# Two hybrid layers in a new order: convolution first, modulation chunks between weight chunks, attention woven into the triangular inverse

## The reference

```python
mod = jax.nn.silu(c) @ ada_w + ada_b          # 6 x 1024 shifts, scales and gates
h = rms_norm(x, norm_mix) * (1 + sc_m) + sh_m
(aq, ak, av, bq, bkc, bvc, bks, bvs, bkw, bvw, bg, cqkv, cz, ca, cb) = jnp.split(h @ w_in, points, axis=-1)
o_a = banded_attention(rope(aq), rope(ak), av, 128, attn_sinks)        # 4 heads of 64
o_b = nsa_mixer(...)    # compressed, selected and window branches, 4 heads of 64, gated by bg
o_c = gated_delta_net(cqkv, ca, cb, cz, conv_w, A_log, dt_bias, gdn_norm)   # 4 heads of 128
x = x + gt_m * (jnp.concatenate([o_a, o_b, o_c], axis=-1) @ w_out)
```

## Time and profile before

| | |
|---|---|
| median of 3 runs | 1755.29 us (1745.7 to 1759.51) |
| profiled execution | 1758.94 us |
| its span, first to last instruction | 1757.1 us |
| TensorE busy | 1564.1 us, 89% |
| TensorE weight loads | 1470.0 us, 84% |
| VectorE busy | 1031.5 us, 59% |
| ScalarE busy | 785.3 us, 45% |
| GpSimd busy | 273.1 us, 16% |
| mean granted TensorE clock | 0.934 of 2.4 GHz |
| first and second hybrid layer's stretch | 43.1 to 273.2 and 534.5 to 758.0 us |

### The profile page before, as it was taken

The page is one execution under the profiler, slowest core; times in us unless marked ns, Lnnn a source line. Parts: engine busy times, 40 slices in busy tenths (PEclk is TensorE's granted clock), DMA queues, the critical chain, the costliest instruction groups (busy, mean ns, idle before and its releaser), DMA issues.

```text
span 1757.1 us, 29189 instructions
## 1 busy us (share of the span) xinstructions
PE 1564.1 (89%) x12266; PEld 1470.0 (84%) x12266; DVE 1031.5 (59%) x1324; ACT 785.3 (45%) x1178; POOL 273.1 (16%) x102
## 2 busy tenths in 40 slices
PE   5899798989898986989999899569999999999997
PEld 2886487989898864879999799448999988889997
DVE  1575536795664765367554533685876454478743
ACT  3335423434234354334533444354664355556642
POOL 0000255570530002554000000220000001100000
PEclk8997798999999988999999899679999999999999
DMA  8358324554453470244445734203553543245442
GB/s 362 145 218 314 122 97 165 205 205 176 180 195 144 180 285 41 97 152 157 176 156 180 258 144 158 96 1 101 187 191 133 198 172 133 98 154 175 161 151 88
DMA packets 30190, 287.82 MB, mean 164 GB/s; under 512 B 2887, under 2 KB 11367, under 8 KB 11784
## 3 DMA queue, kind: packets, MB, share of 16 engines
q1 hardware_dynamic: 28888, 269.51, 41.9%
q0 software_dynamic: 1152, 16.78, 2.4%
q10 hardware_dynamic: 48, 0.05, 0.0%
HBM read 285.23 MB, written 7.39 MB: 167 GB/s over the span
## 4 chain that ended last, share of the span: by engine, by line
PE 72%; DVE 16%; ACT 4%; issue 4%; DMA 3%; POOL 1%; SPq 0%; DVEq 0%; ACTq 0%
PE bank L623 20%; PE bank L624 19%; PE bank L625 19%; DVE w_lo L1676 4%; DMA ring<-w_mix 3%; PE bank L703 2%; DVE arena L1997 2%; ACT w_hi L1253 1%; PE bank L846 1%; PE bank L748 1%; PE bank L836 1%; DVE h L2118 1%; PE bank L844 1%; PE bank L738 1%; PE bank L761 1%
## 5 line engine op out<-in xcount | busy, mean ns | idle before, releaser
L623 PE MATMUL bank<-hi_T,w_hi 128*128 128x256 f32 x2248 | 653.3, 291 | 41.3 <-DVE h_lo L1659 16.4
L1676 DVE TENSOR_TENSOR w_lo<-ring,w_hi 128x2048 fp32r<-128x2048 f32 (+2 forms) x218 | 515.2, 2373 | 229.7 <-ACT w_hi L1253 228.0
L625 PE MATMUL bank<-hi_T,w_lo 128*128 128x256 f32 x2248 | 647.3, 288 | 0.0
L624 PE MATMUL bank<-h_lo,w_hi 128*128 128x256 f32 x2056 | 592.0, 288 | 0.0
L1253 ACT ACTIVATE w_hi<-ring 128x2048 fp32r<-128x2048 f32 (+3 forms) x226 | 391.8, 1735 | 349.6 <-PE bank L625 278.5
L623 PEld LDWEIGHTS bank<-hi_T,w_hi 128*128 128x128 f32 x2248 | 444.1, 198 | 47.7 <-issue 34.8
L625 PEld LDWEIGHTS bank<-hi_T,w_lo 128*128 128x128 f32 x2248 | 443.7, 197 | 0.0
L624 PEld LDWEIGHTS bank<-h_lo,w_hi 128*128 128x128 f32 x2056 | 405.8, 197 | 0.3
L623 PE MATMUL bank<-act_hi,w_hi 128*128 128x256 f32 x704 | 201.3, 286 | 11.7 <-DVE act_lo L1695 9.9
L624 PE MATMUL bank<-act_lo,w_hi 128*128 128x256 f32 x704 | 200.4, 285 | 0.0
L625 PE MATMUL bank<-act_hi,w_lo 128*128 128x256 f32 x704 | 200.3, 284 | 0.0
(11 more groups left out here) (234 smaller groups left out, 2014.6 us busy)
## 6 DMA issues: line engine op xcount, KB each, us to landing
ring<-w_gu SPq DMA_DIRECT2D x22, 2048.0 KB, 8.4
ring<-w_dn SPq DMA_DIRECT2D x32, 1408.0 KB, 6.0
ring<-w_up SPq DMA_DIRECT2D x22, 2048.0 KB, 8.1
ring<-ada SPq DMA_DIRECT2D x16, 2048.0 KB, 8.2
ring<-w_mix SPq DMA_DIRECT2D x12, 2048.0 KB, 8.2
arena<-ada POOLq DMA_DIRECT2D x8, 2048.0 KB, 9.5
ring<-even_in SPq DMA_DIRECT2D x8, 2048.0 KB, 8.3
ring<-odd_in SPq DMA_DIRECT2D x6, 2048.0 KB, 8.3
```

Source lines behind the costliest of these rows:

```text
L623: nc.tensor.matmul(out, wh, xh, start=start, stop=False)
L624: nc.tensor.matmul(out, wh, xl, start=False, stop=False)
L625: return nc.tensor.matmul(out, wl, xh, start=False, stop=stop)
L1676: V.tensor_tensor(w_lo[:, n % SLOTS, at], ring[:, n % SLOTS, at], w_hi[:, u % AHEAD, 0:size].bitcast(F32), ALU.subtract).then_inc(w_lo_rea ...
```

## The change

In both hybrid layers the order is new; the sums computed are the same. The projection is split in `conv{l}` (three chunks for the convolution, now first), `tok{l}`, and `in{l}` (two chunks of attention tiles, and z); the weight columns are permuted on the host to fit. A modulation chunk follows each of the six big chunks, and none is left behind the projection. ScalarE writes the first (rightmost) tap while it takes a convolution tile from PSUM, so that VectorE runs three taps. The convolved rows are transposed between halves of chunks; ScalarE makes the sums of squares and the product with beta from PSUM, where VectorE did. The operand steps move from attention to the projection. Attention's units run inside the seven levels: in level lv TensorE transposes unit lv, and after the updates of X it does the values of unit lv and the scores of unit lv + 2. Scores and transposes of a unit now both use banks 4 and 5. The compression products come behind the projection. The core of the diff, in the order of the file (TensorE, ScalarE, VectorE, GpSimd, host):

```diff
+CN_FIRST, V1_FIRST = 162, 112
...
-    IN_ADA = (2, 4)
     UP, DOWN, OUT = ["columns"] * 11, ["down"] * 8, ["columns"] * 2
     ada_chunks(ADA_FIRST)
     for l in range(L1):
-        phase(f"in{l}", ["columns"] * 5 + ["tokens"], ada_after=IN_ADA)
+        phase(f"conv{l}", ["columns"] * 3, ada_after=(0, 1, 2))
         phase(f"tok{l}", ["rows"], KT * TOKW // 2)
+        phase(f"in{l}", ["columns"] * 2 + ["tokens"], ada_after=(0, 1, 2))
         phase(f"cmp{l}", ["compress"] * 2)
-        ada_chunks(4)
         phase(f"out{l}", OUT)
...
+                U["bank"] = 2 if woven else 4 if name.startswith("hybrid") else 2 * ((len(units) + i) % 2)
...
+                if m >= ADA_FIRST:
+                    pe.wait_ge(acc_ready, m)
...
+                elif U["bank"] == 4:
+                    first = stages["hybrid0"][0] if u < stages["hybrid0"][1] else stages["hybrid1"][0]
+                    if u:
+                        pe.wait_ge(logits_done, u)
+                    if u - first >= 2:
+                        pe.wait_ge(pt_ready, u - 1)
...
+                if units[u]["bank"] == 4:
+                    pe.wait_ge(logits_done, min(u + 2, stages["hybrid0" if u < stages["hybrid0"][1] else "hybrid1"][1]))
...
+            def rotate(l, t):
+
+                pe.wait_ge(gemm_freed, phases[f"in{l}"]["t0"] + t + 1)
+                if t < 2:
+                    pe.wait_ge(gt_copied, 13 * l + 6)
+                elif t < 4:
+                    pe.wait_ge(rope_done, 7 * l + t - 1)
+                else:
+                    pe.wait_ge(g_arg, 3 * l + 3)
+                nc.tensor.matmul(bank[:, 4 + t % 2, 0:S], const("rot"), raw[:, t, :], start=True, stop=True)\
+                    .then_inc(rot_ready, 1)
...
+            def input_columns(l, ready):
+
+                m = ADA_L * l + ADA_FIRST
+                conv_name, name, src = f"conv{l}", f"in{l}", (hi_T, h_lo)
+                columns_chunk(conv_name, 0, 0, src, ready)
+                ada_dots(m)
+                columns_chunk(conv_name, 1, 4, src)
+                ada_dots(m + 1)
+                modulations(m, m + 1)
+                columns_chunk(conv_name, 2, 8, src, parts=(0,))
+                if l == 0:
+                    pe.wait_ge(consts_in, 16 * 2)
+                token_major(l, 0)
+                columns_chunk(conv_name, 2, 8, src, parts=(1,))
+                ada_dots(m + 2)
+                modulations(m + 1, m + 2)
+
...
+                token_major(l, 1)
+
+                columns_chunk(name, 0, 0, src, first_bank=2, parts=(0,))
+                token_major(l, 2)
+                columns_chunk(name, 0, 0, src, first_bank=2, parts=(1,))
+                ada_dots(m + 3)
+                modulations(m + 2, m + 3)
+                rotate(l, 0)
+                rotate(l, 1)
+                columns_chunk(name, 1, 4, src, first_bank=2, parts=(0,))
+                rotate(l, 2)
+                rotate(l, 3)
+                columns_chunk(name, 1, 4, src, first_bank=2, parts=(1,))
+                ada_dots(m + 4)
+                modulations(m + 3, m + 4)
+                log_decays(l)
+                tokens_chunk(name, 2, 8, 2, parts=(0,))
+                rotate(l, 4)
+                rotate(l, 5)
+                tokens_chunk(name, 2, 8, 2, parts=(1,))
+                ada_dots(m + 5)
+                modulations(m + 4, m + 5)
...
+            def mixing(l):
+
+                m = ADA_L * l + ADA_FIRST
+                u0 = stages[f"hybrid{l}"][0]
+
+                pe.wait_ge(xpe_ready, 2 * (l + 1))
+                pe.wait_ge(acc_ready, m + 6)
...
+                    if lv == 1:
+                        modulations(m + 5, m + 6)
+                    transposes(u0 + lv)
...
+                    if lv == 0:
+                        pe.wait_ge(kc_ready, l + 1)
+                    values(u0 + lv)
+                    if lv + 2 < len(range(*stages[f"hybrid{l}"])):
+                        scores(u0 + lv + 2)
...
+            def take_conv(l, t):
+
+                act.wait_ge(gemm_ready, phases[f"conv{l}"]["tile_event"][t])
+                nc.scalar.activation(conv_in[:, t, 3:3 + S], bank[:, t % 4, 0:S], ACT.Copy)
+                nc.scalar.activation(conv[:, t, :], bank[:, t % 4, 0:S], ACT.Copy,
+                                     scale=vec(l, "conv")[:, 36 + t:37 + t]).then_inc(gemm_freed, 1)
...
+                def conv_half(i):
+                    take_conv(l, 2 * i)
+                    take_conv(l, 2 * i + 1)
+                    if i % 2:
+                        ada_rows(m + i // 2)
+                    high(u0 + i + AHEAD)
+
+                def raw_half(i):
+                    for t in (2 * i, 2 * i + 1):
+                        take(name, t, raw[:, t, :], bank[:, (t + 2) % 4, 0:S])
+                    if i % 2:
+                        ada_rows(m + 3 + i // 2)
+                    high(u0 + 8 + i + AHEAD)
+
+                for i in range(4):
+                    conv_half(i)
+                conv_silu(l, 0)
+                conv_half(4)
+                rows_of(l, 0)
+                conv_half(5)
+                conv_silu(l, 1)
+                high(u0 + 6 + AHEAD)
+                for qt in range(QT):
+                    take(f"tok{l}", qt, tokp[:, qt, :], bank[:, qt, 0:TOKW])
...
+                high(u0 + 7 + AHEAD)
+                rows_of(l, 1)
+                conv_silu(l, 2)
+                raw_half(0)
+
+                act.wait_ge(g_arg, 3 * l + 1)
                 nc.scalar.activation(small[:, 64:64 + NCH], small[:, 64:64 + NCH], ACT.Exp)
                 nc.scalar.activation(small[:, 88:92], vec(l, "a_log"), ACT.Exp).then_inc(g_fun, 1)
-                token_major(l, 2, 4)
-                act.wait_ge(g_arg, 4 * l + 2)
+                rows_of(l, 2)
...
+                for i in range(1, 4):
+                    raw_half(i)
...
+                    copy_pt(u0 + lv)
+                    exps(u0 + lv + 1)
+                    if lv >= 5:
+                        late_high(l, lv - 5, lv - 4)
...
+                lows(AHEAD if l else 1, 5)
+                convolution(l, 0)
+                lows(5, 7)
+                convolution(l, 1)
+                lows(7, 9)
+                convolution(l, 2)
+                lows(9, 10)
+                gates(l)
+                lows(10, 11)
...
+                lows(11, 12)
...
+                log_decays(l)
+                unit_rows(l)
+                lows(12, 13)
+                rope(l, 0)
+                rope(l, 1)
+                lows(13, 14)
+                rope(l, 2)
+                rope(l, 3)
+                blocks(l)
+                decays(l)
+                rope(l, 4)
+                rope(l, 5)
+                V.tensor_copy(rot[LO, 6, :], rot[HI, 5, :])
+                V.tensor_copy(rot[HI, 6, :], rot[LO, 5, :]).then_inc(rope_done, 1)
+                decayed(l)
...
+                    recip(u0 + lv + 1)
+                    evac(u0 + lv)
+                    if lv + 2 < len(range(*stages[f"hybrid{l}"])):
+                        logits(u0 + lv + 2)
...
+                for lv in range(LEVELS):
+                    probabilities(u0 + lv)
+                    if lv + 1 < LEVELS:
+                        if lv == 0:
+                            pool.wait_ge(mb_ready, l * LEVELS + 1)
+                        else:
+                            pool.wait_ge(t1_ready, l * 2 * LEVELS + 2 * lv)
+                        lm = const("levels")[:, (lv + 1) * P:(lv + 2) * P]
+                        G.tensor_tensor(MbT[:, (lv + 1) % 2], MT, over(lm, NCH), ALU.mult).then_inc(mb_ready, 1)
+                probabilities(u0 + 7)
...
+        first = np.concatenate([w[:, 1164:2700], first, w[:, 2700:3212]], axis=1)
```

More of the change, by code:

```diff
@@ L43 @@
 GATES, A_COL, B_COL = 256, 268, 272
-KQ_BANKS = (4, 5, 6, 3)
 MOD_COL = 256
@@ L665, in token_tile, with columns_chunk @@
                 return last
-            def columns_chunk(name, nn, j, src, ready=None, after=None):
-                for part in range(2):
+            def columns_chunk(name, nn, j, src, ready=None, first_bank=0, parts=(0, 1)):
+                for part in parts:
                     u = phases[name]["u0"] + 2 * nn + part
@@ new lines, in blocks @@
+            def blocks(l):
+                ch(V.memset(xpe[:, :, :, :], 0.0))
+                dve.wait_ge(gemm_freed, phases[f"in{l}"]["t0"] + 8)
+                for kv, pe_name in enumerate(("pe_k", "pe_v")):
+                    for two, rows in enumerate((LO, HI)):
+                        base = raw[rows, 6 + kv, :].rearrange("p (n q a) -> p a q n", q=8, a=2)[:, two]
+                        for hf in range(2):
+                            last = V.tensor_tensor(
+                                xpe[rows, kv, 8 * hf:8 * hf + 8, 0:N_CMP], base[:, :, hf:hf + N_CMP],
+                                along(vec(l, pe_name)[rows, 8 * hf:8 * hf + 8], N_CMP), ALU.add)
+                    last.then_inc(xpe_ready, 1)
@@ new lines, in convolution @@
+            def convolution(l, part):
```

(25 more changed lines are left out.)

528 lines of the change are left out of this document (221 added, 307 removed).

## The result

The changed kernel takes **1761.28 us** (median of 9 runs, 1755.72 to 1765.32) against 1753.28 for the kernel before beside it (9 runs, 1742.33 to 1759.74): a ratio of **1.0046 [1.0024, 1.0069]**. Timed again with 12 more runs it is 1.0039 [1.0018, 1.0059]. The forecast was 1748, range 1700 to 1785: the range holds the time, and the change is inside the 1% that I called no change, but it lies on the slower side, by 8 us, where 7 us of gain were forecast. The profiled execution took 1762.23 us, with a span of 1760.4.

The account below looks back on a forecast made before the run. TensorE, busy 89% of 1757.1 us, bounds the kernel; attention leaves most room. Layer 1: +36.4 - 51.8 + 13.1 + 2 = -0.3; layer 0: -6.9; so 1751.7 profiled, 1748 at the median, range 1700 to 1785.

Parts of the forecast that it names:

- The levels: Seven delta-net levels with attention woven in: 54.4 us in layer 1, growing by 13.1 from 41.3.
- The rival in which the weave serialises: Attention's steps follow one another in the levels: 10 us a level, 1780; both slower rivals have 0.25 together.
- The projection: Layer 1's projection grows 36.4 us: 17.9 of moved work, the other part stalls from queue order and slow matmuls.
- That they collide: Projection loads land in 11.4 us, not 7.7: 15 us a layer, 1778; both slower rivals have 0.25 together.
- The tail: After the levels, the last unit's copy_pt and values, and late_high, stand ahead of other work: 2 us more.
- GpSimd and VectorE at 0.5 us a layer: Meetings of the two engines in the levels: 0 to 19 us a layer possible, 0.5 taken.
- Layer 0: First hybrid layer takes the same new path, 223.2 us against 230.1.
- The -6.9: Layer 0's gain, 223.2 us against 230.1, whose excess was put mostly on attention at 0.61 of the clock.
- The clock term: In the projection, half clock costs 1.8 us behind each of three long stalls, 5.5 in all.
- The first tap at nothing: Giving the convolution's first tap to ScalarE, and VectorE's remaining taps, both costed at nothing.
- The faster rival: The projection's stalls don't form: 29.3 us less a layer, 1690, or half of it, 1719; chance 0.33.

Follow-up runs that it names:

- the second profile: The changed kernel once more, untouched, with a new profile: ratio 1.0039 to the kernel before.
- small loads: Changed kernel with an eighth of the bytes in each of the six modulation loads between the projection's chunks: 1746.64 us, ratio 0.9945.
- the move of one copy: Changed kernel with ScalarE's copy of conv chunk 1 moved behind the norm's high parts at layer 1's start: 1758.60 us, ratio 1.0017.
- the other two profiles: The kernel before, untouched, profiled a second and third time: spans 1761.9 and 1751.6 us; the second has ratio 1.0012.
- two runs: The convolution's first tap put back on VectorE, in the changed kernel (ratio 1.0029) and in the one with three mended orders (0.9728).
- The version with all three mends: Changed kernel with mix_lo last, SiLUs and convolutions ahead of what waits for loads, and four ropes before the last chunk's w_lo: 1705.34 us, ratio 0.9720.
- the two unforeseen costs out: Changed kernel with mix_lo behind both delta-net columns and the conv chunk 1 copy behind the norm's high parts: 1750.79 us, ratio 0.9986.

## Why the prediction was wrong, step by step

- **The levels: right.** 54.4 forecast, 53.8 measured at clock 0.97, 93% busy. The rival in which the weave serialises is dead.
- **The projection: right in kind and place, nearly in size.** 133.4 for 131.9. The stalls stand where the queues were read to put them; their sum is 21.8 (23.2 in the second profile) for 23.8. The landings on the chain were 10.6, 9.3 and 10.3 us where I had 7.7 with up to 2.4 on top, which moved conv 2 by 1.1 us. That they collide was a rival priced at 15 us a layer, to be decided by a median over 10 us: the median of `w_mix` is 8.9, and small loads gave 7 us a layer, their own sooner landing included. How much of that the forecast already held, with its up to 2.4 us a load, no run separates.
- **The tail: the step that failed.** "`copy_pt` and the values of the last unit, and `late_high`, stand ahead of other work: 2 us more." It is 5.6 us more. Of these, 3.9 are the wait before the last transposes (5.56 for 1.65), which the forecast did not have; the other 1.7 are what it had priced at 2. I went through ScalarE's queue in the tail and not through VectorE's, where `mix_low` had moved in between two steps that TensorE waits for, and I had GpSimd and VectorE at 0.5 us a layer, taking the 1.52 us of a small operation as the size of a meeting. The row beside it shows what it was:

```profile
677.35 2.27 POOL L2192 TENSOR_TENSOR lg<-lg,rec 128x1024 f32<-128x1024 f32 x1 [3.78 <-DVE rec L1724]
```

GpSimd's multiply ended at 679.62 and the small operation, begun at 678.12, at 679.64. A meeting costs the rest of the other engine's instruction, and in the tail GpSimd's last 4.5 us. The tails are 3.6 us over in each layer, 7.2 together, and moving that one subtraction gave 7.6 by the medians and 6.1 in the profile.

- **The start of layer 1: missing.** The change alters the ring's order, and the ring doesn't end at the layer's edge. 2.9 us, once; the move of one copy takes them back in the profile.
- **Layer 0: right by luck.** The -6.9 rested on one execution whose attention ran at 0.61. In the other two profiles layer 0 took 227.2 and 227.5 before; it is 224.9 and 226.1 now. Layer 1 took 227.5 and 223.4 in them. Against the means of the three, layer 0 started 1.8 us too high and layer 1 1.3 too low, so that the sum of both, which the forecast needs, was nearly right because the two errors cancel.
- **The clock term: right in sum.** 5.5 us for three long stalls, 1.8 each. In layer 1 the halves behind those three lost 1.5, 1.2 and 0.9 us, and the one behind the short stall of 2.41, where I had put nothing, 1.6: 5.2 together.
- **The first tap at nothing:** two runs found nothing.
- **The faster rival** asked what the weave gives if the SiLUs stand ahead of the copies: 29.3 us a layer, 1690, half of it 1719. The version with all three mends has 23.4 us less in layer 1's projection, and takes 1705. That rival was a good forecast of another kernel, in which the SiLUs do stand ahead of the copies; in this one they don't.

The account: forecast 1751.7 for a profiled execution, measured 1762.2, 10.5 more: 3.6 in each tail, 2.9 at the start of layer 1, 1.5 in layer 1's projection; the rest, about -1, is within what profiles of one kernel differ. With the two unforeseen costs out the kernel takes 1750.8 for 1748, a ratio of 0.9986 [0.9966, 1.0006] for the forecast's 0.9958; even that version is no gain that can be told, and the 2.8 us are not explained by a run. So where the expected return went is plain: between projection and levels layer 1 saved 51.3 us (71.2 to 19.9), and paid back 12.5 in the levels (41.3 to 53.8) and 37.9 in the projection (95.5 to 133.4), and 5.6 in the tail. Of the 37.9, 13.8 are TensorE's idle time (8.0 to 21.8), nearly all of it queue order; 17.9 are the moved work as priced, and 6.2 are left for slower matmuls.

## What to carry to other kernels

When a stage is woven into another, the gain arrives as waits in the host stage's queues; read each in-order queue item by item for "what stands behind the copy that waits for a load", and expect a second item behind the first that you mend. Look at every VectorE operation with all operands in SBUF for what GpSimd does at that time; its price in these rows is the rest of the instruction that GpSimd has under way. And where a ring's order changes, read the queues of the stage in front too.

## What the runs showed of the hardware that was not expected

- VectorE's and GpSimd's SBUF-to-SBUF operations exclude each other for a whole instruction, in both directions: 5.06 for 1.1 us and 3.98 for 2.28 on VectorE, 3.88 for 1.90 on GpSimd. Whether VectorE could get in between two of GpSimd's instructions no row here shows. VectorE's operations with an operand in PSUM kept their length beside them (0.69 us at 745.38 and 1.13 at 747.67, as in the kernel before).
- A 2 MB load beside another takes 9.3 to 10.6 us here, 7.35 to 7.5 beside one of 256 KB. Two issued 2.5 us apart, at 543.88 and 546.39, were both in at 557.01, 13.1 us after the first, which is less than twice 7.4.
- The same kernel's attention stage ran at granted clocks of 0.58 to 0.75 in layer 1 and 0.61 to 0.74 in layer 0 of three profiles, and its stretches differ by 3 to 4 us from one execution to the next; the stage at 0.58 was only 1.2 us longer than at 0.75. A term that rests on a slow clock in one profile wants a second profile.
